# Additions in groups of eight, the first pair picked by products, and the end of a layer in another order, in a two-layer trunk with a mixture of experts

## The chip, the cores and the metric

The kernel runs on one core of a Trainium2 chip. The metric is the device time of one execution in microseconds (us), the median of several runs.

## The reference

The input x is 512 tokens of 1024 numbers. Two layers follow, each a token mixer and a channel mixer, both behind an RMS norm and added to the residual h:

```python
for i in range(2):
    xn = rms_norm(h, norm_mix[i])
    h = h + (sliding_window_attention(xn, ...) if i == 0 else gated_short_conv(xn, ...))
    h = h + hierarchical_moe(rms_norm(h, norm_ffn[i]), ...)
return rms_norm(h, final_norm)
```

Attention has 16 query and 2 key/value heads of 64 and a window of 128. The short convolution is `[B, C, u] = xn @ w_in`, `y = (B * conv3(C * u)) @ w_out`. The channel mixer picks one of 4 groups of 8 experts for each token and the two best experts in it; each of the 32 experts computes `(silu(x @ w_gate) * (x @ w_up)) @ w_down` with 512 hidden columns, and the results are weighted by the gates and summed. All numbers are float32; the weights of the 64 experts (two layers) are 6 MiB each.

## The kernel before

**Engines and order.** Each engine has its own instruction list, written by hand, and all meet on counting semaphores. Nothing reorders them: the order of the code is the order on the engine. SyncE issues the loads of weights, GpSimd the gathers of rows, TensorE (PE) the products, ScalarE (ACT) and VectorE (DVE) take the results out of the eight PSUM banks.

**Experts.** `experts(l)` exists on every engine. It runs over 16 pairs of experts (`PAIRS`); a pair has 64 slots for each of its two experts (`BLOCK`), so 128 rows. For pair i:

- `select` (L1653, VectorE) writes a 0/1 matrix token x slot from the ranks; `index` (L1121, TensorE, 68 columns) multiplies it by a table and gives the token number, the norm's root and the gate of each slot; `find_pair` takes them out.
- GpSimd's `gather` (L601) fetches the 128 rows of h from DRAM into `picked`. There is one such buffer, so the gather of the next pair waits until `turn_picked` (L1128, eight transposes) has read the last one. `take` (L1685) scales the turned rows into `xg`.
- `gate_up` (L1155) multiplies them by the gate and up weights in four groups of 16 matmul records (an fp32 matmul is two records; the two experts run at once on the two column halves of the array). `last_quarter` is the fourth group.
- `swish`, `hidden` (L1695), `turn_hidden` (L1173) and `take_hidden` (L795) make the turned hidden rows; `down` (L1180) multiplies them by the down weights in two halves, `down_first` and `down_last`, with `turn_picked` of the next pair between them.
- `take_high` (L804) and `take_low` (L1710) split the scaled result in two fp32r parts, `spread` (L1141) and `find_slots` (L1704) make the way back from slots to tokens, and `combine` (L1147, four matmuls) gives what is added to one tile of 128 tokens. VectorE adds it to h (L1747). The four tiles of pair i-1 are combined between the four `gate_up` groups of pair i, all through banks 0 and 1.

**Weights.** A pair has six pieces of 2 MiB (`PIECES`): two for k 0 to 3 of gate/up, two for k 4 to 7, two for down. They go round nine slots (`RING`). Nine are loaded before the stage begins; each later one (L467) waits until the piece nine before it has been used: `gu_done` counts the ends of a pair's first and second half of gate/up, `down_done` those of down. So the tenth piece waits for the first `gu_done` of the layer.

**Start of the experts.** `router` ends with the ranks (L1627, L1629). Then VectorE selects pair 0, TensorE multiplies (L1121), VectorE makes the row numbers (L1659), GpSimd gathers; beside it TensorE counts (L1115), turns the ranks (L1135), multiplies the table of the gates and the index of pair 1, and runs two filler matmuls (`keep_busy`, L901) before it turns the picked rows and starts `gate_up`.

**End of layer 0.** After the last pair the eight half tiles are added to h, four low halves and then four high halves (`add_last`, L1726). Each engine then reads the fullest expert's count and skips the branch for experts with over 64 tokens. TensorE turns h in 32 transposes (`turn_half`, L936), ScalarE copies them out in high parts (L674), VectorE in low parts (L1401); ScalarE (L843) and VectorE (L1839) split the weights of the convolution's column blocks in high and low parts, block 0 step by step, block 1 as a whole. `split_product` (L943) then runs over eight blocks, block j from the j-th split on. ScalarE's order is: split 0, four even copies, splits 1 to 3, four odd copies, splits 4 to 7, four roots (L659), the eight splits of block 1.

**End of layer 1.** `norm(4)` takes four tiles: ScalarE the roots (L659), VectorE the product with root and gain (L1392), SyncE stores.

## Time and profile before

| | us |
|---|---|
| median of 3 runs | 1353.9 (1350.97 to 1355.2) |
| the profiled execution | 1351.3 |
| its span, first to last instruction | 1349.4 |
| TensorE busy | 1294.5 (96%) |
| VectorE busy | 578.0 (43%) |
| ScalarE busy | 256.7 (19%) |
| GpSimd busy | 110.4 (8%) |
| granted TensorE clock, mean | 0.988 |

The span is cut by the work into the attention and first router (to about 188), the experts of layer 0 (199 to 661), the convolution and second router (667 to 865), the experts of layer 1 (875 to 1340) and the last norm. An engine that is busy 96% of the span can still wait for something at the one place that sets the end of a stage, so the table alone does not say what bounds the kernel. A matmul's busy time is partly modelled; start to start of a long group is the safer reading.

### The profile page before, as it was taken

The numbers are of one execution on the slowest core, as the hardware profiler recorded it, in microseconds if no ns is written. First come the engines' busy times: TensorE is split into PE (matmuls) and PEld (weight loads), VectorE is DVE, ScalarE is ACT, GpSimd is POOL, SyncE is SP. The second block draws the span as 40 slices with busy tenths as digits, with TensorE's granted clock in tenths as the row PEclk, the third lists the DMA queues.
The fourth block names the chain that finished last, engine by engine and source line by source line (L and its number), as shares of the span: only waits on it lengthen the run. The fifth ranks groups of instructions, "written<-read, shape, count | busy, mean of one in ns | idle before, by whom it ended". The sixth has DMA issues, their size and how long they took to land.

```text
span 1349.4 us, 14705 instructions
## 1 busy us (share of the span) xinstructions
PE 1294.5 (96%) x5986; PEld 668.7 (50%) x5986; DVE 578.0 (43%) x1232; ACT 256.7 (19%) x556; POOL 110.4 (8%) x120
## 2 busy tenths in 40 slices
PE   7999989999999999999999999899999999999996
PEld 5777653344334444333588888633443333443332
DVE  5586342343343333333566661423433433433334
ACT  3257611010100111000532221110101001101002
POOL 3850010000000000000000000100000000000000
PEclk8999989999999999999999999899999999999998
DMA  9301768999999999999723337589999999999993
GB/s 346 97 1 52 307 279 357 427 427 428 426 425 427 426 426 427 426 428 428 213 94 105 113 149 294 221 342 426 427 427 427 427 426 425 427 426 426 426 428 150
DMA packets 65306, 450.73 MB, mean 334 GB/s; under 512 B 17722, under 2 KB 33108, under 8 KB 40660
## 3 DMA queue, kind: packets, MB, share of 16 engines
q1 hardware_dynamic: 58976, 436.09, 78.0%
q0 software_dynamic: 5760, 12.59, 2.5%
q8 instruction: 50, 0.82, 0.2%
q10 hardware_dynamic: 500, 1.06, 0.2%
q14 instruction: 20, 0.16, 0.0%
HBM read 451.79 MB, written 6.32 MB: 339 GB/s over the span
## 4 chain that ended last, share of the span: by engine, by line
PE 83%; DMA 10%; DVE 4%; ACT 1%; issue 1%; DVEq 0%; SPq 0%; ACTq 0%
PE ps L1155 29%; PE ps L943 20%; PE ps L1180 15%; PE ps L1147 9%; DMA big<-in_moe_w_gate_up_dram 7%; DMA small<-in_moe_w_gate_up_dram 2%; PE ps L1128 2%; PE ps L1086 1%; PE ps L901 1%; PE ps L1121 1%; PE ps L1025 1%; PE ps L1141 1%; PE ps L992 1%; ACT arena L795 1%; DVE h L1726 1%
## 5 line engine op out<-in xcount | busy, mean ns | idle before, releaser
L1155 PE MATMUL ps<-big,arena 128*64 128x512 f32 x1200 | 464.8, 597 | 5.1 <-DMA big<-in_moe_w_gate_up_dram 1.9
L1747 DVE TENSOR_TENSOR h<-ps,h 128x512 f32<-128x512 f32 x240 | 154.7, 686 | 203.7 <-PE ps L1147 203.7
L1155 PEld LDWEIGHTS ps<-big,arena 128*64 128x64 f32 x1200 | 133.5, 136 | 144.4 <-issue 143.2
L1180 PE MATMUL ps<-small,arena 128*64 128x512 f32 x336 | 152.7, 597 | 3.3 <-ACT arena L795 3.1
L1155 PE MATMUL ps<-small,arena 128*64 128x512 f32 x336 | 152.7, 597 | 1.1 <-DMA big<-in_moe_w_gate_up_dram 1.1
L1147 PE MATMUL ps<-arena_parts 128*128 128x512 f32 x512 | 151.4, 419 | 1.7 <-DVE arena_parts L1710 1.7
L1147 PEld LDWEIGHTS ps<-arena_parts 128*128 128x128 f32 x512 | 86.6, 188 | 95.6 <-issue 83.8
L943 PE MATMUL ps<-xt_parts,small_parts 128*128 128x512 f32 x288 | 111.5, 397 | 2.9 <-DVE big_parts L1839 2.9
L790 ACT ACTIVATE gain<-ps,slot_root 128x512 f32<-128x512 f32 x32 | 22.0, 688 | 477.9 <-PE ps L1155 477.9
L943 PE MATMUL ps<-xr_parts,small_parts 128*128 128x512 f32 x272 | 106.6, 392 | 0.0
L943 PE MATMUL ps<-xt_parts,big_parts 128*128 128x512 f32 x256 | 99.7, 389 | 0.0
L601 POOL DMA_INDIRECT arena<-h_rows,arena x32 | 32.4, 1012 | 801.2 <-PE ps L1128 762.4
L1685 DVE TENSOR_TENSOR arena<-ps,gffn 128x512 f32<-128x512 f32 x64 | 41.3, 686 | 118.0 <-PE ps L1128 118.0
L804 ACT ACTIVATE arena_parts<-ps,slot_gate 128x512 fp32r<-128x512 f32 x64 | 44.0, 687 | 238.7 <-PE ps L1180 238.7
L1710 DVE SCALAR_TENSOR_TENSOR arena_parts<-ps,slot_gate,arena_parts 128x512 fp32r<-128x512 f32 x64 | 48.1, 751 | 94.1 <-ACT arena_parts L804 94.1
L1180 PE MATMUL ps<-arena 128*64 128x512 f32 x176 | 79.8, 597 | 1.7 <-ACT arena L795 1.4
L1180 PE MATMUL ps<-xr,arena 128*64 128x512 f32 x176 | 79.8, 597 | 1.7 <-ACT arena L795 1.4
L1155 PE MATMUL ps<-xr,arena 128*64 128x512 f32 x176 | 79.7, 597 | 0.5 <-DMA big<-in_moe_w_gate_up_dram 0.5
L1180 PE MATMUL ps<-xt,arena 128*64 128x512 f32 x176 | 80.0, 598 | 0.0
L1155 PE MATMUL ps<-arena 128*64 128x512 f32 x176 | 79.8, 597 | 0.0
L1695 DVE SCALAR_TENSOR_TENSOR gain<-ps,slot_root,gain 128x256 f32<-128x256 f32 x64 | 37.6, 670 | 90.4 <-PE ps L1155 71.6
L1180 PE MATMUL ps<-big,arena 128*64 128x512 f32 x160 | 72.7, 597 | 3.3 <-ACT arena L795 3.1
(208 smaller groups left out, 1646.6 us busy)
## 6 DMA issues: line engine op xcount, KB each, us to landing
big<-in_moe_w_gate_up_dram SPq DMA_DIRECT2D x75, 2048.0 KB, 22.9
small<-in_moe_w_gate_up_dram SPq DMA_DIRECT2D x21, 2048.0 KB, 21.7
small<-in_moe_w_down_dram SPq DMA_DIRECT2D x21, 2048.0 KB, 24.7
arena<-in_moe_w_gate_up_dram SPq DMA_DIRECT2D x11, 2048.0 KB, 22.0
xr<-in_moe_w_down_dram SPq DMA_DIRECT2D x11, 2048.0 KB, 23.7
xt<-in_moe_w_down_dram SPq DMA_DIRECT2D x11, 2048.0 KB, 23.3
arena<-in_moe_w_down_dram SPq DMA_DIRECT2D x11, 2048.0 KB, 24.6
xr<-in_moe_w_gate_up_dram SPq DMA_DIRECT2D x11, 2048.0 KB, 22.4
```

The lines of the kernel that those rows point to most:

```text
L601: nc.gpsimd.indirect_dma_start(out=picked, out_offset=None, in_=h_dram[l], in_offset=bass.IndirectOffsetOnAxis(ap=where[:, slot:slot + 1], ...
L790: nc.scalar.activation(silu, ps[2][:], ACT.Silu, scale=slot_root[:, slot:slot + 1]).then_inc(S.silu_ready, 1)
L804: nc.scalar.activation(parts(y_high[:, c, :]), ps[6 + c][:], ACT.Copy, scale=slot_gate[:, slot:slot + 1]).then_inc(S.high_ready, 1)
L943: mm = nc.tensor.matmul(bank, parts(a), parts(b), start=start and a is left and b is right, stop=stop and a is left_low)
L1128: mm = nc.tensor.transpose(ps[d // 4][:, (d % 4) * P:(d % 4 + 1) * P], picked.rearrange("p (q k) -> p k q", k=DT)[:, d, :], ident[:])
L1147: mm = nc.tensor.matmul(ps[bank + n][:], parts(selT[:, slot, t * P:(t + 1) * P]), parts(y[:, c, :]), start=y is y_high, stop=y is y_low)
L1155: mm = nc.tensor.matmul(ps[2 + half][j * BLOCK:(j + 1) * BLOCK, :], xg[:, k, j * BLOCK:(j + 1) * BLOCK], ws[j][:, k % FT, half * FF:(half ...
L1180: mm = nc.tensor.matmul(ps[6 + c][j * BLOCK:(j + 1) * BLOCK, :], hidT[:, k, j * BLOCK:(j + 1) * BLOCK], ws[j][:, k, c * HALF:(c + 1) * HAL ...
L1685: V.tensor_tensor(xg[:, ks, :], ps[half][:].rearrange("p (a b) -> p a b", a=4), layer_gain[0][:, ks].unsqueeze(2).to_broadcast([P, 4, P]), ...
L1695: V.scalar_tensor_tensor(out=hid.rearrange("q (k p) -> q p k", p=P)[:, :, ks], in0=ps[3][:].rearrange("q (p k) -> q p k", p=P)[:, :, ks], ...
L1710: V.scalar_tensor_tensor(out=parts(y_low[:, c, :]), in0=ps[6 + c][:], scalar=slot_gate[:, slot:slot + 1], in1=parts(y_high[:, c, :]), op0= ...
L1747: ins = V.tensor_tensor(hs, ps[c][:], hs, ALU.add)
```

## The change

1. **Pairs.** `gate_up` of k 0 to 3 is one group of 32 records, then come `spread` and the additions of tiles 0 and 1 of the pair before (eight matmuls, banks 0, 1 and 6, 7), 16 records, tiles 2 and 3 (eight), the last quarter, `turn_picked` of the next pair, `index`, `turn_hidden`, and then `down` in one piece.
2. **First pair of a layer.** A second selection, plain fp32, is written to `first_sel`. `pick_first` multiplies h by it: for each of eight k, four matmuls of 128x128. This gives the picked and turned rows with no gather. Index, ranks, counts and the index of pair 1 move behind the first 32 records of `gate_up` (`first_indexes`), the filler matmuls are gone, and the gather of pair 1 is the first of the layer. The first index and the gates' index become one.
3. **End of layer 0.** VectorE reads the count before the last additions. It then adds the low halves, splits step 0, takes the even turns, splits 1, adds the high halves, splits 2 and 3, takes the odd turns and splits 4 to 7. TensorE turns the even halves, runs the first 18 products, and then turns the odd halves.
4. **End of layer 1.** GpSimd multiplies tiles 0 and 1 of h by the gain, VectorE by the root.
5. Some semaphores are merged (`rel_in` into `attn_in`, `w_o_in` into `w_out_in`, `eps_ready` into `consts_ready`).

```diff
@@ pe: first pair
+            def pick_first(S, l):
+
+                pe.wait_ge(first_selected, l + 1)
+                for k in range(DT):
+                    for t in range(TT):
+                        mm = nc.tensor.matmul(ps[k // 4][:, k % 4 * P:(k % 4 + 1) * P],
+                                              h[:, t, :].rearrange("p (q k) -> p k q", k=DT)[:, k, :], first_sel[:, t, :],
+                                              start=(t == 0), stop=(t == TT - 1))
+                    if k % 4 == 3:
+                        mm.then_inc(S.picked_turned, 1)
+
+            def first_indexes(S, l):
+
+                o = l * PAIRS
+                pe.wait_ge(S.selected, o + 1)
+                pe.wait_ge(tab_ready, l + 1)
+                index(S)
+                turn_ranks()
+                count(l)
+                pe.wait_ge(S.selected, o + 2)
+                index(S)
+                pe.wait_ge(ranks_taken, l + 1)
...
@@ pe: experts
-                pe.wait_ge(S.selected, o + 1)
-                index(S, 0, GATE)
-                count(l)
-                turn_ranks()
-                pe.wait_ge(tab_ready, l + 1)
-                index(S, GATE, TAB)
-                pe.wait_ge(S.selected, o + 2)
-                index(S)
-                keep_busy(2, 3)
-                pe.wait_ge(S.picked_in, 16 * (o + 1))
-                turn_picked(S)
+                pick_first(S, l)
...
+                    ws = weights(i, 0)
                     pe.wait_ge(S.rows_taken, 2 * n + 1)
-                    ws = weights(i, 0)
-                    gate_up(both((0, 1)), ws)
+                    gate_up(both((0, 1, 2, 3)), ws).then_inc(S.gu_done, 1)
                     if i == 0:
-                        pe.wait_ge(ranks_taken, l + 1)
+                        first_indexes(S, l)
                     spread(S, n, i)
                     if i:
-                        add_pair(i - 1, 0)
+                        add_tiles(i - 1, (0, 1))
+                    ws = weights(i, 2)
                     pe.wait_ge(S.rows_taken, 2 * n + 2)
-                    gate_up(both((2, 3)), ws).then_inc(S.gu_done, 1)
-                    if i:
-                        add_pair(i - 1, 1)
-                    ws = weights(i, 2)
                     gate_up(both((4, 5)), ws)
                     if i:
-                        add_pair(i - 1, 2)
+                        add_tiles(i - 1, (2, 3))
                     last_quarter(S, ws)
-                    if i:
-                        add_pair(i - 1, 3)
+                    if i < LAST:
+                        if i:
+                            pe.wait_ge(S.added, l * ADDS + TT * (i - 1) + 3)
+                        pe.wait_ge(S.picked_in, 16 * (l * LAST + i + 1))
+                        turn_picked(S)
...
                     turn_hidden(S, n)
                     ws = weights(i, 4)
-                    down_first(S, n, ws)
-                    if i < LAST:
-                        if i:
-                            pe.wait_ge(S.added, l * ADDS + TT * i)
-                        pe.wait_ge(S.picked_in, 16 * (n + 2))
-                        turn_picked(S)
-                    down_last(S, n, ws)
+                    down(S, n, ws)
...
@@ pe: convolution, block 0
-            for half in range(2):
-                for t in range(TT):
-                    turn_half(t, half)
+            for t in range(TT):
+                turn_half(t, 0)
...
+                        if k == 2:
+                            for t in range(TT):
+                                turn_half(t, 1)
...
@@ dve: router
+                V.tensor_tensor(first_sel.rearrange("p t (j s) -> p t j s", j=2),
+                                iota[:].unsqueeze(1).unsqueeze(1).to_broadcast([P, TT, 2, BLOCK]),
+                                rank[:, :, 0:2].unsqueeze(3).to_broadcast([P, TT, 2, BLOCK]), ALU.is_equal)\
+                    .then_inc(first_selected, 1)
                 select(main, slice(0, 2))
...
@@ dve: end of layer 0
+                def conv_begin(between_halves):
+                    split_low_of(CONV_SPLIT, 0, [0])
+                    for t in range(TT):
+                        take_turned(2, t, [0])
+                    split_low_of(CONV_SPLIT + 1, 0, [1])
+                    between_halves()
+                    for k in (2, 3):
+                        split_low_of(CONV_SPLIT + k, 0, [k])
+                    for t in range(TT):
+                        take_turned(2, t, [1])
+                    for k in range(FT, DT):
+                        split_low_of(CONV_SPLIT + k, 0, [k])
...
@@ dve: norm_tile
+                if i == 4 and t < 2:
+                    dve.wait_ge(pool_scaled, t + 1)
+                    V.tensor_scalar(xr[:, t, :], xr[:, t, :], rstd[:, t:t + 1], None, ALU.mult).then_inc(xr_ready, 1)
+                    return
...
@@ gpsimd
-                    gather(S, l, n, i % AHEAD, 2 * n if i else None)
+                    if i:
+                        gather(S, l, n, i % AHEAD, 2 * n)
+                    else:
+                        pool.wait_ge(S.index_ready, n + 1)
...
+            for t in range(2):
+                pool.wait_ge(h_ready, 2 * (TT + t + 1))
+                nc.gpsimd.tensor_tensor(xr[:, t, :], h[:, t, :], gain[:], ALU.mult).then_inc(pool_scaled, 1)
```

TensorE, start of layer 0's experts before: the last matmuls of the router, then index, counts, ranks, filler, turned rows, and the first gate products.

```order
L1107 MATMUL ps<-arena,ones 128x32
L901 MATMUL ps<-ident 128x512
L1121 MATMUL ps<-arena_parts 128x4 x4
L1115 MATMUL ps<-arena,ones 128x32 x4
L1135 MATMUL ps<-ident,rank 32x128 x4
L1121 MATMUL ps<-arena_parts 128x64 x4
L1121 MATMUL ps<-arena_parts 128x68 x4
L901 MATMUL ps<-ident 128x512 x2
L1128 MATMUL ps<-ident,arena 128x128 x8
L1155 MATMUL ps<-big,arena 64x512
```

The same place in the change (its lines are numbered anew: L1144 is `pick_first`, L1184 `gate_up`).

```order
L1113 MATMUL ps<-arena,ones 128x32
L908 MATMUL ps<-ident 128x512
L1144 MATMUL ps<-arena,h 128x128 x32
L1184 MATMUL ps<-big,arena 64x512
...
L1127 MATMUL ps<-arena_parts 128x68 x4
L1164 MATMUL ps<-ident,rank 32x128 x4
L1121 MATMUL ps<-arena,ones 128x32 x4
L1127 MATMUL ps<-arena_parts 128x68 x4
L1170 MATMUL ps<-arena_parts 128x512
```

The index products, ranks and counts have moved behind the first sixteen gate products; 32 fp32 products stand in the place of the turned rows.

VectorE, from the last additions of layer 0 to the splits of block 1, before (the branch for full experts left out).

```order
L1726 TENSOR_TENSOR h<-ps,h 128x512 x7
...
L1401 TENSOR_TENSOR xr_parts<-ps,xt_parts 128x512 x4
L1839 SCALAR_TENSOR_TENSOR big_parts<-big,gmix,small_parts 128x3x128 x4
L1401 TENSOR_TENSOR xr_parts<-ps,xt_parts 128x512 x4
L1839 SCALAR_TENSOR_TENSOR big_parts<-big,gmix,small_parts 128x3x128 x4
...
L1839 SCALAR_TENSOR_TENSOR big_parts<-big,gmix,small_parts 128x3x128 x8
```

And in the change (L1753 additions, L1671 splits, L1422 turned parts).

```order
L1753 TENSOR_TENSOR h<-ps,h 128x512 x3
L1671 SCALAR_TENSOR_TENSOR big_parts<-big,gmix,small_parts 128x3x128
L1422 TENSOR_TENSOR xr_parts<-ps,xt_parts 128x512 x4
L1671 SCALAR_TENSOR_TENSOR big_parts<-big,gmix,small_parts 128x3x128
L1753 TENSOR_TENSOR h<-ps,h 128x512 x4
L1671 SCALAR_TENSOR_TENSOR big_parts<-big,gmix,small_parts 128x3x128 x2
L1422 TENSOR_TENSOR xr_parts<-ps,xt_parts 128x512 x4
L1671 SCALAR_TENSOR_TENSOR big_parts<-big,gmix,small_parts 128x3x128 x4
...
L1671 SCALAR_TENSOR_TENSOR big_parts<-big,gmix,small_parts 128x3x128 x8
```

The four additions of the high halves have moved behind the even turned parts, and one split ahead of them. ScalarE's list is not changed here.

## Rows read from the trace of the kernel before

**Rows 1.** Busy time (us) of each engine in long stretches, clock, DMA share, GB/s

```profile
208.50:628.50 420.00, 411.57 (x1876) 166.36 (x1872) 155.04 (x284) 42.01 (x76) 18.33 (x28) 1.00 1.01 426
884.50:1305.00 420.50, 411.73 (x1876) 166.59 (x1872) 155.08 (x284) 42.29 (x76) 18.33 (x28) 1.00 1.01 426
```

**Rows 2.** The chain that ended last: start us, us, what

```profile
224.31 3.43 PE ps L1155 x16
...
583.04 1.14 PE ps L1147 x4
584.18 3.58 PE ps L1155 x16
...
598.49 30.38 DMA small<-in_moe_w_gate_up_dram
...
629.00 3.65 PE ps L1155 x16
...
684.71 144.21 PE ps L943 x636
```

**Rows 3.** Timeline of SyncE's queue, tenth piece of each layer

```profile
206.98 0.33 SPq L467 DMA_DIRECT2D big<-in_moe_w_gate_up_dram  x1
...
883.05 0.33 SPq L467 DMA_DIRECT2D big<-in_moe_w_gate_up_dram  x1
```

**Rows 4.** Timeline, start of the experts: start us, us, engine line op

```profile
187.41 0.69 DVE L1653 TENSOR_TENSOR arena_parts<-iota,rank 128x512 fp32r<-128x512 f32 x1
188.15 0.61 PE L1121 MATMUL ps<-arena_parts 128*128 128x4 f32 x4 [0.43 <-DVE arena_parts L1653]
188.62 1.06 PE L1115 MATMUL ps<-arena,ones 128*128 128x32 f32 x8
...
189.51 0.60 PE L1135 MATMUL ps<-ident,rank 128*32 128x128 f32 x4
...
199.27 0.64 PE L1155 MATMUL ps<-big,arena 128*64 128x512 f32 x1 [0.42 <-DVE arena L1685]
...
864.59 0.69 DVE L1653 TENSOR_TENSOR arena_parts<-iota,rank 128x512 fp32r<-128x512 f32 x1
```

**Rows 5.** One us of windows; the number before the last two is the granted clock

```profile
197.00:198.00 1.00, 1.00 (x3) 0.40 (x3) 0.00 (x0) 0.00 (x0) 0.00 (x0) 0.51 0.02 8
```

**Rows 6.** Turns in the timeline, and fp32 products grouped by line

```profile
660.69 3.65 PE L936 MATMUL ps<-ident,h 128*128 128x128 f32 x32
...
L1335 PE MATMUL ps<-gain,ones 128*128 128x128 f32 x8 | 1.1, 275 | 0.0
```

**Rows 7.** Landing of the gathers started at 190.0, at 221.6, and of all 32

```profile
L601 POOL DMA_INDIRECT arena<-h_rows,arena x1: 1074/1074/1074, 190.0 to 190.0; - x1
...
DMA to landing us min/median/max: 7.6/7.6/7.6
...
DMA to landing us min/median/max: 10.2/10.2/10.2
...
DMA to landing us min/median/max: 3.4/11.1/12.3
```

**Rows 8.** Timeline, end of layer 0

```profile
664.09 2.48 DVE L1401 TENSOR_TENSOR xr_parts<-ps,xt_parts 128x512 fp32r<-128x512 f32 x4 [1.23 <-ACT xt_parts L674]
664.76 2.08 ACT L674 ACTIVATE xt_parts<-ps 128x512 fp32r<-128x512 f32 x4
...
667.24 0.47 PE L943 MATMUL ps<-xt_parts,small_parts 128*128 128x512 f32 x1 [2.90 <-DVE big_parts L1839]
...
678.41 4.33 DVE L1839 SCALAR_TENSOR_TENSOR big_parts<-big,gmix,small_parts 128x384 fp32r<-128x384 f32 x8 [2.90 <-ACT small_parts L843]
```

**Rows 9.** A product on GpSimd by line, and the load of the last gain

```profile
L582 POOL TENSOR_TENSOR h<-h,arena 128x1024 f32<-128x1024 f32 x4 | 11.5, 2896 | 0.0
...
gain<-in_final_norm_dram ACTq DMA_DIRECT2D x1, 512.0 KB, 3.8
```

**Rows 10.** Timeline of VectorE in the last norm

```profile
1340.63 0.16 DVE L1387 RECIPROCAL rstd<-rstd 128x1 f32<-128x1 f32 x1 [0.89 <-ACT rstd L666]
...
1345.01 1.29 DVE L1392 SCALAR_TENSOR_TENSOR xr<-h,rstd,gain 128x1024 f32<-128x1024 f32 x1
```

More of the change, by code:

```diff
@@ L1174, in turn_hidden, with down_steps @@
                     mm.then_inc(S.turned, 1)
-            def down(S, steps, ws):
+            def down_steps(steps, ws):
                 for k, c in steps:
@@ L1641, in router, with split_low_of @@
                     .then_inc(tab_ready, 1)
-                dve.wait_ge(rank_ps, 2 * l + 2)
-                V.tensor_reduce(most_f[:], ps[7][:, 0:E], X, ALU.max).then_inc(dve_step, 1)
-                steps[0] += 1
-                dve.wait_ge(dve_step, steps[0])
-                V.tensor_copy(fullest[:, l:l + 1], most_f[:]).then_inc(route_ready, 1)
+            def split_low_of(n, j, ks):
+                dve.wait_ge(w_high, n + 1)
+                w, high = conv_weights(j)
+                for k in ks:
+                    at = slice(3 * k, 3 * k + 3)
+                    ins = V.scalar_tensor_tensor(out=parts(w[:, at]), in0=w[:, at], scalar=gmix[:, k:k + 1],
+                                                 in1=parts(high[:, at]), op0=ALU.mult, op1=ALU.subtract)
+                ins.then_inc(w_split, 1)
             layer_gain = [None]
@@ L1760, in experts, with last_halves @@
                     if i:
[L1761 to L1762 removed]
+                        add_tile(i - 1, 2, 0)
+                        add_tile(i - 1, 3, 6)
                     hidden(S, n, i % AHEAD)
[L1764 to L1768 removed]
                     if i < LAST:
                         take(S, n + 1)
[L1771 to L1773 removed]
+                    if i + 2 < PAIRS:
+                        dve.wait_ge(S.indexed, o + i + 3)
+                        find_pair(S, i + 2)
+                def last_halves():
+                    n = o + LAST
+                    count = before + ADDS
                     take_low(S, n, 0, LAST % AHEAD)
@@ L1778, in experts, with last_other_halves, last_tiles @@
                         add_last(count + t + 1, t, 0)
+                def last_other_halves():
                     for t in range(TT):
-                        add_last(count + TT + t + 1, t, 1)
-                else:
+                        add_last(before + ADDS + TT + t + 1, t, 1)
+                def last_tiles():
+                    n = o + LAST
                     for c in range(2):
@@ L1785, in experts @@
                         for c in range(2):
-                            add_last(count + 2 * t + c + 1, t, c)
-                dve.wait_ge(h_ready, 2 * TT * (l + 1))
+                            add_last(before + ADDS + 2 * t + c + 1, t, c)
+                def conv_begin(between_halves):
[10 more added lines that the diff above has]
+                        split_low_of(CONV_SPLIT + k, 0, [k])
                 dve.wait_ge(route_ready, l + 1)
```

125 lines of the change are left out of this document (56 added, 69 removed).

## The prediction

> **What bounds the kernel now.** I read the busy shares of long windows first, then the chain of waits, then the starts and ends of the stages in the timeline. TensorE is busy 96% of the span, yet in the two expert stages it is not the bound. From 208.5 to 628.5 us, and again from 884.5 to 1305, the DMA engines are at their full share at 426 GB/s [rows 1]. TensorE leads in the middle of a stage, because nine pieces of weights were loaded ahead, and has used its lead up at the end: the chain of waits runs 30.38 us through one weight transfer and comes back to TensorE at 629.00, at the last pair [rows 2]. A piece is 2.097 MB, so 4.92 us at 426 GB/s. The tenth piece, the first that needs a slot to come free, is issued at 206.98 [rows 3]; the last pair's products start 422.0 later. In layer 1 that piece goes out at 883.05. The end of an expert stage therefore hangs on when its tenth piece is issued, and on whether the queue ever runs dry behind it. Elsewhere TensorE bounds; the stretches to look at are the start of the experts and the end of layer 0.
>
> **Groups of eight, down in one piece: 0 us.** A group of 16 product records takes 3.58 between additions and 3.43 where nothing changes before it; four additions take 1.14, of which four records of 512 columns (half of 3.43/8 each) are 0.86 [rows 2]. A change to the additions and back so costs about 0.43. The change takes out two a pair, some 0.8 us, 26 over 32 pairs. I count it as nothing: TensorE only reaches its transfers earlier. Its cover is the stream of 422 us; were that gone, all 26 would show. In the last pair, behind the last transfer, two changes less are worth 0.8, but no addition lies beside the hidden rows any more, which VectorE makes in about as long. Zero.
>
> **First pair by products.** Before, the first selection of layer 0 starts at 187.41 and the first gate product at 199.27; between them lie index products, a gather and filler products [rows 4]. After: one more selection of the same shape (0.69), then 32 fp32 products, 64 records of 128x128. No such product is in the trace of before. The nearest rows are 32 turns of 128x128 in 3.65, 0.114 each, and eight fp32 records of this very shape in 1.1, 0.1375 each with their tail [rows 6]. From below, a 512-column record holds its half of the array 0.43 (eight twos in 3.43), a quarter of it is 0.107. I take 0.114, the steady one: 7.3 us (6.8 to 8.8). Start 188.15, end 195.45. The 32 records of gate products follow in 7.05 (the second half of the picked rows is only awaited later), and piece ten is issued at 202.6 instead of 206.98: 4.4 earlier. In layer 1 the selection at 864.59 gives 872.6 and 879.75 instead of 883.05: 3.3 earlier.
>
> What was ahead of the first product is now behind it, on TensorE: index 0.6, turned ranks 0.6, counts 1.06, index 0.6, together 2.9 [rows 4], then the spread (0.4) and 7.0 of products. So the next two pieces are issued 10.35 after the tenth, where two pieces last 9.83: 0.5 us of empty queue. Then TensorE stands at the picked rows of pair 1. Their gather needs the second index, whose product ends near 205.4, and starts 1.2 behind it (before: 188.76 to 190.0 [rows 4, 7]), at 206.6. Landings of before: 3.4 on an empty queue; 7.6 for the first gather, whose stream drained at about 196.5; 10.2 where new pieces came 2.8 after its start; 11.1 as the median [rows 7]. Here the pieces ahead of it drain at 202.6 + 1.5 + 9.8 = 213.9 (full traffic comes 1.5 after the issue [rows 1, 3]) and new ones come only after. That is nearest to the 7.6 row, which landed 1.1 after the drain: 215.0, a landing of 8.4. TensorE wants the rows at 212.85: **a wait of 2.2 us** that no profile of before has. Bounds: none with 3.4, 4.8 with 11.1.
>
> Behind that wait stand the turns 1.1, index 0.4, hidden turns with their wait 1.0 and down 7.05, and the issue of the next pieces. Down is done 22.1 after the tenth piece's issue, where four pieces last 19.66. The stream starts in effect 2.45 after 202.6, at 205.05: **1.95 earlier than before in layer 0**, and at 882.2 against 883.05, **0.85 earlier in layer 1**. Later gathers are issued a pair ahead and cost nothing.
>
> The Trainium skill ("DMA: Bandwidth & Descriptors", Queues, rings and completion order) says that each DMA engine goes round between the queue rows packet by packet. By that rule the gather would hardly wait for the pieces, and the sum below would be 3.9 lower. The 10.2 and 11.1 of the rows speak against it.
>
> **Tail of layer 0.** VectorE now does its first weight split and the even turns before the second half of the additions. Before: idle 1.23 behind the additions, even turns from 664.09 in 2.48, first split, convolution from 667.24 [rows 8]. After: four additions fewer ahead of them, first split to 661.0, even turns from the first copy at 661.9 to 664.4. TensorE starts 2.75 earlier. It then has 16 of the 32 turns inside the run (1.8), so block 0 ends at 683.0 instead of 683.8. But ScalarE's order is unchanged: its odd copies stand ahead of its last four splits, its four roots and the eight splits of block 1. The odd turns now come behind 18 products, at 668.6; the odd copies start at about 669.2 instead of 664.76, so the eight splits end at 682.9 instead of 678.4, and VectorE's eight (4.33) at 687.25. Block 1 waits for all of them. It began at 684.71 [rows 2, 8]: **2.6 us later**. TensorE ran 144 us without a wait from there [rows 2], so nothing gives it back. SyncE's bias and weight loads wait for all additions and move about 4.6 too, ahead of their use by as much as they lose.
>
> **Tail of layer 1.** GpSimd multiplies two tiles by the gain; its nearest product, 128x1024, takes 2.9 us [rows 9]. The gain takes 3.8 to land [rows 9], at about 1337.0, so the second tile stands at 1342.8; then VectorE needs one short product and its two full tiles, to 1346.8. Before it ended at 1346.3, after an idle 0.89 behind the branch, which now stands earlier [rows 10]. From +0.5 at this price to -0.9 if GpSimd is never awaited; I take zero. Merged semaphores: zero, since TensorE waits for weights there.
>
> **Sum**: -1.95 + 2.6 - 0.85 = -0.2, on the profiled execution's own 1351.3: 1351.1. The median of the runs is 1353.9, 2.6 above that execution; the forecast for the median is **1353.7 us**. A measurement of this kernel can tell about 0.3% (4.1 us) from no change, so: no change.
>
> **Rivals.**
> - *Full gather wait* (slower). If the gather lands as in the loaded stage, in 11.1, the wait is 4.8 and the streams start 0.65 and 1.75 later than before, not earlier: with the 2.6, +5.0, 1358.9. For it: most gathers take this long. Against: they have a backlog of four pieces or more. It decides from a landing of 10.6 on. Chance 0.19.
> - *No gather wait*: the queue lets the gather through, as the rule above has it; streams 3.9 and 2.8 earlier, tail +2.6: -4.1, 1349.8. Without the late block 1 too (its splits ready in time), -7.5, 1346.4. For it: 3.4 on an empty queue. Against: 7.6 with one and a half pieces of backlog. Chance 0.26 for the two.
> - *The products at half clock.* The granted clock was at its half level at 197 [rows 5], after sparse small products. At that level picking takes twice 7.3: +14.6, 1368. Against: before, the clock was full until 191, and TensorE is now dense from 188. Chance 0.04.
> - *TensorE is the bound after all*: -26, 1328. Against it rows 1 and 2. Chance 0.03.
>
> **Numbers.** The forecast case has 0.48 and runs from -2.9 (gather 7.6, 0.107 a record) to +4.3 (gather 9.2, 0.1375). The range takes in most of the first two rivals: 1348.0 to 1359.5. Faster by over 0.3%: half of the no-wait rival's first part, all of its second, the TensorE case and a little of the forecast, 0.25. Slower: the full wait, the half clock and the forecast's dear end, 0.25. Within: 0.50.
>
> **What would show it.** Picking: 64 records in 7 to 9 us from 188.1. In both layers a TensorE idle time of about 2 us before the turned rows of pair 1. A pair in mid-stage about 0.8 shorter, the waits for weights some pairs earlier, and the last of them 424.5 behind the issue of piece ten. An idle time near 3 us before block 1, ended by VectorE's splits. It is wrong if the last wait for weights moves by more than the stream's start does, if pair 1's rows land with TensorE still busy, or if block 1 starts before 684.

## The result, and the profile after

| | before | after |
|---|---|---|
| median, us (4 runs each) | 1352.97 (1350.97 to 1355.2) | 1374.47 (1372.02 to 1376.83) |
| ratio, 95% interval | | 1.0158 (1.0131 to 1.0185) |
| span of the profiled execution, us | 1349.4 | 1374.0 |
| mean granted clock of TensorE | 0.988 | 0.987 |

The change made the kernel 21.5 us slower. The forecast, no change in 1348.0 to 1359.5, was wrong.

The chain of waits of the kernel after holds most of it. The columns are start and length in us, then what ran. First the start of the experts in layer 0 and the last pair there:

```profile
187.20 0.70 DVE arena L1651
187.94 15.48 PE ps L1144 x64
...
214.29 9.54 DMA arena<-h_rows,arena
...
226.56 8.06 PE ps L1209 x32
...
636.53 7.09 PE ps L1184 x32
```

Picking the first pair (L1144) takes 15.48 us for 64 records, 0.242 each; the forecast had 7.3. Then the gather of pair 1 is on the chain, and the down products behind it take 8.06 where the later pairs take 7.09. The same chain in layer 1:

```profile
877.92 15.48 PE ps L1144 x64
...
904.20 11.37 DMA arena<-h_rows,arena
...
915.61 1.97 PE ps L1134 x8
...
919.34 8.13 PE ps L1209 x32
...
1329.45 7.09 PE ps L1184 x32
```

Here the gather takes 11.37, the turns behind it 1.97 instead of 1.09, and down 8.13. TensorE's timeline has the two waits, in brackets; the forecast had 2.2 for each:

```profile
223.87 1.16 PE L1134 MATMUL ps<-ident,arena 128*128 128x128 f32 x8 [3.31 <-DMA arena<-h_rows,arena]
...
915.61 1.97 PE L1134 MATMUL ps<-ident,arena 128*128 128x128 f32 x8 [5.08 <-DMA arena<-h_rows,arena]
```

SyncE's queue, from the tenth piece on, answers to [rows 3]:

```profile
210.49 0.33 SPq L466 DMA_DIRECT2D big<-in_moe_w_gate_up_dram  x1
...
220.60 0.33 SPq L466 DMA_DIRECT2D arena<-in_moe_w_down_dram  x1
...
234.66 0.33 SPq L466 DMA_DIRECT2D xr<-in_moe_w_gate_up_dram  x1
...
900.46 0.33 SPq L466 DMA_DIRECT2D big<-in_moe_w_gate_up_dram  x1
...
910.58 0.33 SPq L466 DMA_DIRECT2D xr<-in_moe_w_down_dram  x1
...
927.50 0.33 SPq L466 DMA_DIRECT2D arena<-in_moe_w_gate_up_dram  x1
```

The tenth piece goes out 3.5 later than before in layer 0 (206.98) and 17.4 later in layer 1 (883.05); it was to go out 4.4 and 3.3 earlier. Between the second and the third of these issues lie 14.1 and 16.9 us, for two pieces that last 9.8. Between these marks the DMA engines are still at their full share, by the windows (busy us of each engine, granted clock, DMA share, GB/s), which answer to [rows 1]:

```profile
216.00:636.00 420.00, 402.31 (x1872) 178.75 (x1868) 151.86 (x284) 42.29 (x76) 18.35 (x28) 1.00 1.00 423
908.00:1329.00 421.00, 401.43 (x1862) 179.06 (x1858) 152.10 (x285) 42.29 (x76) 18.36 (x28) 0.99 1.00 421
```

The end of layer 0, from the chain again, answers to [rows 8] and to the 684.71 144.21 of [rows 2]:

```profile
672.49 4.40 PE ps L950 x18
...
677.37 2.07 ACT xt_parts L681 x4
...
686.91 4.06 ACT small_parts L850 x8
691.00 4.33 DVE big_parts L1671 x8
695.37 146.09 PE ps L950 x636
```

From the odd turns on, the chain goes through ScalarE's copies, its last four splits, its roots and its eight splits of block 1, then VectorE's eight. TensorE's timeline and the windows around the start of block 1 show what that does to it (the number before the last two is the granted clock).

```profile
695.37 0.50 PE L950 MATMUL ps<-xt_parts,small_parts 128*128 128x512 f32 x1 [3.54 <-DVE big_parts L1671]
```

```profile
690.00:695.00 5.00, 1.83 (x13) 1.47 (x11) 4.00 (x8) 4.09 (x8) 0.00 (x0) 1.00 0.13 42
695.00:700.00 5.00, 4.63 (x13) 3.71 (x14) 4.79 (x10) 1.62 (x4) 0.00 (x0) 0.66 0.00 0
```

TensorE idles 3.54 us, and then the clock is down for some 3 us. The 636 records of the convolution take 146.09 instead of 144.21.

With these marks both profiled executions split into the same intervals. "Rank known" is the start of the first selection (187.41 and 864.59 before, [rows 4]; 187.20 and 877.17 after).

| interval | before | after | difference | forecast |
|---|---|---|---|---|
| start to rank known, layer 0 | 187.41 | 187.20 | -0.2 | 0 |
| rank known to tenth piece, layer 0 | 19.57 | 23.29 | +3.7 | -4.4 |
| tenth piece to last pair's products, layer 0 | 422.02 | 426.04 | +4.0 | +2.45 |
| last pair's products to block 1 | 55.71 | 58.84 | +3.1 | +2.6 |
| block 1 to rank known, layer 1 | 179.88 | 181.80 | +1.9 | 0 |
| rank known to tenth piece, layer 1 | 18.46 | 23.29 | +4.8 | -3.3 |
| tenth piece to last pair's products, layer 1 | 422.17 | 428.99 | +6.8 | +2.45 |
| last pair's products to the end | 44.18 | 44.55 | +0.4 | 0 |

They add to the 24.6 between the spans, up to rounding. Spans of single executions scatter by some us, so the experiments are compared by the medians of their runs, and their profiles by these intervals.

### The profile page after: what moved, and what is told of

It is laid out like the page before. It is cut to its first block, busy times and chain, and to the rows that moved or that the text cites. A ratio compares the mean times of both kernels' runs of the same rounds, so it can differ in the third digit from the quotient of the medians.

```text
span 1374.0 us, 14898 instructions
## 1 busy us (share of the span) xinstructions
PE 1299.1 (95%) x6082; PEld 721.4 (53%) x6082; DVE 573.1 (42%) x1234; ACT 256.9 (19%) x556; POOL 113.1 (8%) x120
## 4 chain that ended last, share of the span: by engine, by line
PE 89%; DVE 3%; issue 3%; ACT 2%; DMA 2%; SPq 0%; POOLq 0%; DVEq 0%
PE ps L1184 32%; PE ps L950 19%; PE ps L1209 17%; PE ps L1176 9%; PE ps L1134 2%; PE ps L1144 2%; DMA arena<-h_rows,arena 2%; PE ps L1092 1%; PE ps L1031 1%; PE ps L1127 1%; PE ps L1170 1%; ACT arena L802 1%; PE ps L998 1%; PE ps L1202 1%; PE ps L1018 1%
## 5 line engine op out<-in xcount | busy, mean ns | idle before, releaser
L1184 PE MATMUL ps<-big,arena 128*64 128x512 f32 x1200 | 458.6, 595 | 16.0 <-issue 16.0
L1184 PEld LDWEIGHTS ps<-big,arena 128*64 128x64 f32 x1200 | 139.6, 137 | 151.3 <-issue 151.0
L1777 DVE TENSOR_TENSOR h<-ps,h 128x512 f32<-128x512 f32 x240 | 148.9, 683 | 95.5 <-PE ps L1176 95.5
L1209 PE MATMUL ps<-small,arena 128*64 128x512 f32 x336 | 149.4, 598 | 3.3 <-ACT arena L802 3.1
L1184 PE MATMUL ps<-small,arena 128*64 128x512 f32 x336 | 150.4, 595 | 1.3 <-issue 1.3
L1176 PE MATMUL ps<-arena_parts 128*128 128x512 f32 x512 | 134.7, 405 | 1.7 <-DVE arena_parts L1737 1.7
L1176 PEld LDWEIGHTS ps<-arena_parts 128*128 128x128 f32 x512 | 91.2, 188 | 52.4 <-issue 35.1
L1731 DVE TENSOR_SCALAR arena_parts<-ps,slot_id 128x512 fp32r<-128x512 f32 x32 | 24.0, 750 | 193.0 <-PE ps L1170 193.0
L1184 PE MATMUL ps<-xr,arena 128*64 128x512 f32 x176 | 78.7, 596 | 0.5 <-issue 0.5
L1184 PE MATMUL ps<-arena 128*64 128x512 f32 x176 | 78.7, 596 | 0.5 <-issue 0.5
L1209 PE MATMUL ps<-xt,arena 128*64 128x512 f32 x176 | 78.9, 601 | 0.0
L1184 PE MATMUL ps<-xt,arena 128*64 128x512 f32 x160 | 72.8, 598 | 2.4 <-issue 2.4
L1209 PE MATMUL ps<-big,arena 128*64 128x512 f32 x160 | 70.5, 593 | 3.3 <-ACT arena L802 3.1
```

What stands on the lines that cost most here:

```text
L1176: mm = nc.tensor.matmul(ps[bank + n][:], parts(selT[:, slot, t * P:(t + 1) * P]), parts(y[:, c, :]), start=y is y_high, stop=y is y_low)
L1184: mm = nc.tensor.matmul(ps[2 + half][j * BLOCK:(j + 1) * BLOCK, :], xg[:, k, j * BLOCK:(j + 1) * BLOCK], ws[j][:, k % FT, half * FF:(half ...
L1209: mm = nc.tensor.matmul(ps[6 + c][j * BLOCK:(j + 1) * BLOCK, :], hidT[:, k, j * BLOCK:(j + 1) * BLOCK], ws[j][:, k, c * HALF:(c + 1) * HAL ...
L1731: V.tensor_scalar(parts(selT[:, slot, :]), ps[4][:], slot_id[:, 0:1], None, ALU.is_equal)\
L1777: ins = V.tensor_tensor(hs, ps[bank + c][:], hs, ALU.add)
```

## The experiments

Twelve kernels ran, in four groups, each beside the kernel before. Its medians there were 1353.99, 1352.87, 1353.3 and 1354.09.

**1. The picking with contiguous columns.** The stationary operand of a picking product is every eighth column of h. Here it is 128 neighbouring ones. The first pair of each layer so works on permuted columns, and what lies behind it gets other numbers.

```
-     h[:, t, :].rearrange("p (q k) -> p k q", k=DT)[:, k, :], first_sel[:, t, :],
+     h[:, t, k * P:(k + 1) * P], first_sel[:, t, :],
```

> The changed kernel, with the 32 picking products reading 128 neighbouring columns of h as their stationary operand instead of every eighth one (so the first pair of each layer gets other rows of its input than it should). Theory A, the stride of the stationary operand doubles a product record: the 64 records take about 7.3 us instead of 15.5 in both layers, the tenth piece goes out about 8 earlier in each, and the median falls by some 16 us, to about 1358. Theory B, an fp32 product of this shape costs 0.24 a record however its operand lies: 15.5 us stay and so does the median, 1374. The wait for the gather of pair 1 stays in both, 3 to 5 us.

Measured: 1360.71 us (10 runs), ratio 1.0056 (1.0041 to 1.0071). That is 13.8 us under the kernel after, with the order of addresses as the only edit, and 2.7 above the 1358 expected. The chain of this kernel, in both layers:

```profile
186.72 7.41 PE ps L1144 x64
...
866.88 7.41 PE ps L1144 x64
```

The 64 records take 7.41, 0.116 each, within 0.1 of the forecast's 7.3. Rank known to tenth piece is 15.22 in both layers, as forecast (15.2). The tenth piece to the last pair's products, however, takes 424.7 and 428.7, not 422: the wait for the gather is left. Picking is then still no gain over the kernel before.

**2. The price of a stride by itself.** At the end of the kernel before, series of 16 products of 128x128 fp32 with the columns of h at a stride, each product two records. They only add work.

```
+ for n in range(16):
+     nc.tensor.matmul(ps[7][:, 0:P], flat[n % 4].rearrange("p (q k) -> p k q", k=8)[:, n // 4, :],
+                      ident[:], start=True, stop=True)
...
```

> The kernel before, with eight series of 16 products of 128x128 appended on TensorE behind its last use (they change no output): fp32 with the stationary operand at stride 1, 2, 4 and 8 elements, turns at stride 1 and 8, and fp32 with the moving operand at stride 8 and 1. Theory A (stride of the stationary operand): 0.11 us a record at stride 1, growing with the stride to 0.24 at 8, turns 0.11 to 0.14 whatever the stride. Theory B (shape): 0.24 in all the fp32 series with changing weights.

One execution, with the granted clock at 1.00 throughout the series. TensorE's timeline of this kernel:

```profile
1351.18 3.73 PE L1376 MATMUL ps<-ident,h 128*128 128x128 f32 x32
1354.75 3.93 PE L1378 MATMUL ps<-ident,h 128*128 128x128 f32 x32
1358.52 7.63 PE L1380 MATMUL ps<-ident,h 128*128 128x128 f32 x32
1365.98 7.77 PE L1382 MATMUL ps<-ident,h 128*128 128x128 f32 x32
1373.59 1.91 PE L1384 MATMUL ps<-ident,h 128*128 128x128 f32 x16
1375.34 1.95 PE L1386 MATMUL ps<-ident,h 128*128 128x128 f32 x16
1377.12 7.62 PE L1388 MATMUL ps<-h,ident 128*128 128x128 f32 x32
1384.57 3.75 PE L1390 MATMUL ps<-h,ident 128*128 128x128 f32 x32
```

L1376 to L1382 have h as the stationary operand at strides 1, 2, 4 and 8: 0.117, 0.123, 0.238 and 0.243 a record. L1388 and L1390 have it as the moving operand at strides 8 and 1: 0.238 and 0.117. L1384 and L1386 are turns at strides 1 and 8, 0.119 and 0.122. So a stride of 4 or 8 elements doubles an fp32 product for the stationary operand, a stride of 8 does so for the moving one too, and a turn at stride 8 stays as it is. Theory A of the expectation held for the turns; between the strides it had a growth, where the series show one step between 2 and 4.

**3. The start of the kernel before in the kernel after.** Gather of the first pair, filler and index products as before; groups of eight, tails and norm of the change.

```
-                 pick_first(S, l)
+                 pe.wait_ge(S.selected, o + 1)
+                 index(S, 0, GATE)
...
+                 keep_busy(2, 3)
+                 pe.wait_ge(S.picked_in, 16 * (o + 1))
+                 turn_picked(S)
```

> The changed kernel with the start of a layer's experts as before it (index products first, gather, turned rows, no picking products). If the picking products and the order around them are what costs, and the grouping of a pair costs nothing because the weight stream of some 422 us bounds the stage, the last wait for weights of each layer stands 422 us behind the tenth piece again and the whole is before plus the tail of layer 0 (3 us) plus at most 2: 1356 to 1358. Rival, the grouping itself costs: 1362 or more, with the distance from the tenth piece to the last wait clearly over 422.

Measured: 1357.05 (10 runs), ratio 1.0027 (1.0017 to 1.0036), as expected. So picking as it was made costs 17.4 against this start, and with contiguous columns 3.7. The tenth piece to the last pair's products is back at 422.1 and 422.2.

**4. The indexes ahead of the picking.** This starts the gather of pair 1 on an empty DMA queue, and so takes the gather's wait away. VectorE scales the picked rows (`take`) behind the index work here, no longer ahead of it.

```
+                 first_indexes(S, l)
                  pick_first(S, l)
...
-                    if i == 0:
-                        first_indexes(S, l)
```

> The changed kernel with the index products, ranks and counts ahead of the picking products again, so that the gather of pair 1 starts about 10 us before it is needed. The tenth piece goes out about 3.5 later than in the changed kernel, but the TensorE waits of 3.3 and 5.1 us before the turned rows of pair 1 vanish and the later pieces follow without a gap. By the theory that four slots' issues hang on that wait: effective stream start 1 us earlier in layer 0, 4 earlier in layer 1, median about 1370. Rival, the wait is hidden behind the stream and only the start counts: 7 us slower, 1381.

Measured: 1379.12 (4 runs), ratio 1.0195 (1.0169 to 1.0222), near the 1381 of the rival and not the 1370 of the theory. What failed was the price of the start, not the end of the wait: the gathers of pair 1 and pair 2 in layer 0 landed in 3.3 and 11.0 us,

```profile
L600 POOL DMA_INDIRECT arena<-h_rows,arena x2: 1029/1052/1074, 196.2 to 228.4; - x2
...
DMA to landing us min/median/max: 3.3/7.2/11.0
```

and the tenth piece to the last products is 422.18 and 422.05, so the wait's 3.9 and 6.9 are gone. But rank known to tenth piece went from 23.29 to 29.8: the indexes need selections and gates on VectorE and 4.3 us of small products on TensorE (1.04, 0.85, 1.55 and 0.86), all now ahead of the first big one. I had counted on 3.5, and on TensorE alone. So the rival's number came out, but not by its reason: the wait was not hidden before, and it did go.

**5. Groups of eight and down in one piece**, on the kernel before. The kernel has part 1 of the change, and two small things with it: the merged semaphores of part 5, and VectorE's reading of the fullest expert's count ahead of the last additions, from part 3.

```
-                    gate_up(both((0, 1)), ws)
+                    gate_up(both((0, 1, 2, 3)), ws).then_inc(S.gu_done, 1)
...
-                    down_first(S, n, ws)
+                    down(S, n, ws)
```

> The kernel before with part 1 alone (additions in two groups of eight, down in one piece); start of the experts, layer 0's tail and the last norm as before. Theory: part 1 is worth nothing, since the weights' stream sets the 422 us between a layer's tenth piece and the last pair's products. Tenth piece at 207 and 883 as before, last pair's products at 629 and 1305 (+-1), 1352 to 1356 us, ratio 1.000 +-0.002. Rival (part 1 costs something that the first pair's experiments hid): last pair's products over 2 us later than 629 at the same tenth piece. Rival (TensorE bound): 26 us less in all.

Measured: 1350.13 (12 runs), ratio 0.9977 (0.9969 to 0.9986): faster by 2.7 us, under 0.3%, but with an interval that leaves out 1. The 1352 to 1356 expected is missed by 2; the stream theory holds, to 0.3 us. SyncE's queue and the chain:

```profile
205.48 0.33 SPq L467 DMA_DIRECT2D big<-in_moe_w_gate_up_dram  x1
...
880.24 0.33 SPq L467 DMA_DIRECT2D big<-in_moe_w_gate_up_dram  x1
```

```profile
627.49 7.09 PE ps L1177 x32
...
682.38 144.21 PE ps L943 x636
...
1302.07 7.09 PE ps L1177 x32
```

Tenth piece to last products is 422.01 and 421.83. The gain lies outside: the spread no longer stands before the tenth piece's release (rank known to tenth piece 18.60 and 17.97 for 19.57 and 18.46; the first gate product to the tenth piece 7.12 in both layers for 7.71 and 7.70), and from the last pair's products to block 1 it takes 54.89 for 55.71. The latter is not the last pair's own gain: its products to the first of the last eight additions take 28.80 for 28.33. Behind the additions, VectorE stood 1.23 idle before the even turned parts [rows 8], while it read the count; that idle time is gone. So part 1 by itself is worth less than the 2.7; how much, no run separates.

**6. Layer 0's new tail added to it** (the last norm stays as before).

```
-            for half in range(2):
-                for t in range(TT):
-                    turn_half(t, half)
+            for t in range(TT):
+                turn_half(t, 0)
...
+                        if k == 2:
+                            for t in range(TT):
+                                turn_half(t, 1)
```

> The last kernel (part 1 alone) with layer 0's new tail added; the last norm stays as before. Theory: the new order on ScalarE (odd copies of the turned rows ahead of splits 4 to 7, roots ahead of block 1) makes block 1's matmuls late: they begin 3 us later than in the kernel before (687 to 688 against 684.7), and the whole is 3 to 5 us longer than the last kernel, ratio to before 1.002 to 1.004. Rival: the tail costs nothing and what after lost there came from the late start: block 1 at 685, same time as the last kernel.

Measured: 1356.93 (12 runs), ratio 1.0027 (1.0017 to 1.0036), 6.8 above the fifth kernel, where 3 to 5 were expected. The last products to block 1 take 60.43 (54.89 without), the same idle of 3.54 stands before block 1, and the convolution takes 146.07 for 144.21. Block 1 begins at 689.73, not at 687 to 688. This kernel differs from the third in the last norm alone, and the two ratios are the same.

**7. The same tail with block 1 served first.** ScalarE makes splits 4 to 7 before the odd copies, and block 1 before the roots; VectorE takes block 1's low parts ahead of the zeroing and the roots.

```
-            for k in range(1, FT):
+            for k in range(1, DT):
                 split_high_of(0, [k])
             for t in range(TT):
                 take_turned(2, t, [1])
-            for k in range(FT, DT):
-                split_high_of(0, [k])
+            split_conv(1)
             for t in range(TT):
                 root(2, t)
 
-            split_conv(1)
```

> The last kernel with three moves: on ScalarE splits 4 to 7 stand ahead of the odd copies and block 1 ahead of the roots, on VectorE block 1's low parts ahead of the zeroing and roots. Theory (ScalarE's and VectorE's order makes block 1 late): block 1's matmuls begin at 682 to 685, and 3 or more us are won against the last kernel: 1350 to 1354 us, ratio to before 0.997 to 1.001. Rival (the loads of block 1's weights or TensorE itself set it): block 1 as late as in the last kernel, same time.

Measured: 1349.76 (11 runs), ratio 0.9973 (0.9964 to 0.9982), 7.2 below the sixth. The chain has no ScalarE piece in the run of products any more, and the convolution is back at its old length:

```profile
677.03 12.30 PE ps L941 x54
...
690.22 144.21 PE ps L941 x636
```

Block 1 began later than expected on the clock (690.22 against 682 to 685), since this execution's tenth piece went out at 210.99 already; from its last products on it took 56.88. That is 2.0 more than in the fifth kernel, and the stretch from block 1 to the known rank is 1.6 shorter (178.26 for 179.89). The order on the two engines was the cause; which of the three moves counts was not separated. With it mended the new tail is level with the old one (1350.13) and no better.

**8. The last norm alone**, on the kernel before.

```
+                if i == 4 and t < 2:
+                    dve.wait_ge(pool_scaled, t + 1)
+                    V.tensor_scalar(xr[:, t, :], xr[:, t, :], rstd[:, t:t + 1], None, ALU.mult).then_inc(xr_ready, 1)
+                    return
```

> The kernel before with part 4 alone (last norm: GpSimd multiplies the gain into two of the four row tiles). My forecast's term was 0 with both bounds small: 1353.5 +-1 us, ratio 1.000 +-0.001. Rival: the end of layer 1 is 1 us or more shorter or longer.

Measured: 1353.54 (12 runs), ratio 0.9994 (0.9983 to 1.0006). Nothing, as forecast.

**9 and 10. The fifth kernel without filler products.** In layer 1 they run past the landing of the first gather. The ninth kernel drops them in both layers, the tenth in layer 1 alone.

```
-                keep_busy(2, 3)
+                if l == 0:
+                    keep_busy(2, 3)
```

> Part 1 alone (as in the groups kernel), and the two filler matmuls ahead of the wait for the first pair's gather are gone in both layers. Theory: in layer 1 the filler ran from 868.3 to 871.6 at half clock while the gathered rows had landed at about 868.9, so it holds the stream back by up to 2.6 us; in layer 0 the gather landed last (196.7) and the filler cost nothing. So rank known to tenth piece falls from 18.0 to 15.5 to 17 in layer 1 and stays at 18.6 in layer 0, and the time falls by 1 to 2.5 us against the groups kernel (1350.1): 1347.5 to 1349.5. Rival: the longer idle time lets the granted clock fall for the first pair's turns and gate/up, and 1 to 4 us are lost in each layer: 1352 to 1357.

> As the last kernel, but the filler stays in layer 0 and is gone in layer 1 alone. Theory: same as the last kernel or up to 1 us below it (in layer 0 the filler only keeps the clock up through a wait for the gather). Rival: as the groups kernel or above it, if the clock falls in layer 1 too.

Measured: ninth 1351.12 (11 runs), ratio 0.9982 (0.9969 to 0.9994); tenth 1349.16 (7 runs), ratio 0.9969 (0.9957 to 0.9982). The ninth lies above its 1347.5 to 1349.5 and below its rival's 1352 to 1357, the tenth 2.0 below the ninth, where up to 1 was expected. The intervals overlap with the fifth's (0.9977), so no gain over it is shown. The chains of layer 1, of the fifth kernel (with two filler products, L901) and of the tenth, show why:

```profile
868.33 3.23 PE ps L901 x4
871.56 0.71 PE ps L1127 x4
...
873.12 7.09 PE ps L1177 x32
```

```profile
869.97 1.97 PE ps L1127 x8
...
871.96 9.13 PE ps L1177 x32
```

Without filler the turns start 1.6 us earlier on the clock and 2.7 nearer to the known rank (6.5 behind it for 9.3), but run at half clock, and the first products take 9.13 for 7.09. Rank known to tenth piece is 17.7 for 17.97: the wait's gain went into the clock. In layer 0 of the ninth kernel it is 20.85 for 18.60, since there the gather landed last anyway and only the clock was lost. From the last products to block 1 the ninth's profile has 57.01, where the same code took 54.89 and 54.93 in the fifth and the tenth: such an interval can differ by 2 us between single executions.

**11 and 12. Filler during the wait for pair 1's gather**, on the first kernel (contiguous columns): ten filler products, then four.

```
+                        if i == 0:
+                            keep_busy(10, 0)
                         pe.wait_ge(S.picked_in, 16 * (l * LAST + i + 1))
```

> The kernel of the first experiment (after's picking with contiguous columns, so the first pair gets other rows), with ten filler matmuls ahead of the wait for pair 1's gather, so TensorE does not sit idle there. Theory of the gather wait in two parts, the wait itself and the clock that falls behind it (turns 1.97 us for 1.09, down 8.50 for 7.09 in layer 1): the clock stays at 1.00, turns take 1.09 and down 7.09, and 2 us of the 6.6 that layer 1's stream lost to the wait come back; nothing in layer 0 (its clock had not fallen): 1357 to 1360 against 1360.7, ratio to before 1.003 to 1.005. Rival: the filler outlasts the gather or delays it and the time is the same or longer.

Measured: 1364.60 (5 runs), ratio 1.0091 (1.0077 to 1.0104). Missed: ten are 8.78 us where the first kernel's waits are 3.2 and 4.4, and both layers take some 430 from tenth piece to last products. The rival of this expectation held.

> As the busy wait kernel, with four filler matmuls in place of ten. The ten took 8.78 us (0.878 each) and outlasted the gather; four take 3.5 us and end about when the gather of pair 1 lands (waits of 3.3 to 4.4 us without filler). Theory (part of the gather wait's price is the clock that falls behind it): the clock stays at 1.00, in layer 1 turns take 1.09 for 1.97 and down 7.09 for 8.50, tenth piece to last pair's products falls from 428.7 to 426 to 427.5 there and stays at 424.7 in layer 0; 1358 to 1360 against 1360.7, ratio to before 1.003 to 1.005. Rival (only the wait itself counts, the weights' queue had run dry by then anyway): 428.7 again and the same time as the first experiment, 1360 to 1361.

Measured: 1357.03 (12 runs), ratio 1.0028 (1.0014 to 1.0041), 3.7 under the first kernel (the two intervals meet at 1.0041) and 1 below the 1358 to 1360 expected. Layer 1's chain, of the first kernel and of this one:

```profile
885.10 10.68 DMA arena<-h_rows,arena
...
895.82 1.97 PE ps L1134 x8
...
899.55 8.50 PE ps L1209 x32
```

```profile
887.47 11.03 DMA arena<-h_rows,arena
...
898.55 1.16 PE ps L1134 x8
...
900.91 7.09 PE ps L1209 x32
```

The gather took no less, but what follows runs at full clock, and tenth piece to last products fell from 428.65 to 426.12. In layer 0, where the clock had not fallen, it is 425.11 for 424.68. The two intervals account for 2.1 of the 3.7. The windows say what a late issue of pieces means. In the first kernel and in this one:

```profile
905.00:910.00 5.00, 5.00 (x26) 1.74 (x24) 1.50 (x2) 1.37 (x2) 0.00 (x0) 1.00 0.25 59
```

```profile
905.00:910.00 5.00, 5.00 (x26) 1.96 (x24) 1.50 (x2) 1.37 (x2) 0.00 (x0) 1.00 0.56 174
```

The DMA share falls to 0.25 and 0.56 for five us: in part of that stretch the queue was empty. With the fillers, picking with contiguous columns is level with the start of the kernel before (the third kernel's 1.0027), not better.

By medians, as ratios to before times 1353: part 1 with the count read ahead -3.1; the rest of layer 0's tail +6.8; the norm 0; picking with its gather's wait +3.9; the stride in it +13.8. That is +21.4. These are the steps from one kernel to the next (before, fifth, sixth, third, first, after), so they add up by construction; what they show is the size of each step. The fourth kernel bears out the wait, and the seventh the tail.

## Why the prediction was wrong

- **What bounds the stages: right.** Eight kernels without a late gather gave 421.8 to 422.4 us from the tenth piece to the last pair's products, with the additions in four groups or in two. A pair in mid-stage became shorter as forecast (its down products start at 255.45 and 283.37, 27.92 apart for 28.64 before), and in the later pairs TensorE stood idle ahead of its first products instead (1.26 before the last pair's, at 635.28).
- **Groups and down in one piece, "0 us": nearly right.** The fifth kernel measured -2.7. In its profile some 0.6 a layer lie in the spread's place, which I had not counted, and 0.8 in layer 0's end, by the count read ahead of the additions. The last pair itself gained nothing, as I had it.
- **First pair by products, 7.3 us (6.8 to 8.8): this step failed.** It took 15.48 in each layer. I priced the record by its shape, from turns and from products whose stationary operand lies in neighbouring columns [rows 6], and took no account of the eighth-column view in the added line. The first experiment gave 7.41 with that view gone, the second the price of the stride. The turns were the nearest row and could not warn: those of L936 in [rows 6] read neighbouring columns, and the second experiment shows that turns do not pay for the stride of 8 either. Even the half-clock rival (twice 7.3 a layer) lay under it. The miss is 8.2 us a layer, 16.4 of the profile's 24.6.
- **Wait for pair 1's gather: mechanism right, size too small.** The streams were to lose 2.45 a layer behind the tenth piece and lost 4.0 and 6.8. The landing was 9.5 and 11.4, not 8.4: the next two pieces were issued 10.1 behind the tenth, 6.3 behind the gather's start, and before it had landed. Whether that is why it landed late was not separated, nor why layer 1 is slower: four kernels with this start have 9.4 to 9.5 in layer 0 and 10.7 to 11.4 in layer 1. And I priced the wait without the clock that falls behind it. The "full gather wait" rival, 0.19, held in layer 1 (a wait of 5.08 for its 4.8) and lies further off than the forecast's landing in layer 0. The Trainium skill ("DMA: Bandwidth & Descriptors", Queues, rings and completion order) has each DMA engine alternate between queue rows by packets. Read as "the gather hardly waits" this is not what these runs show (3.3 on an empty queue in the fourth kernel, 9.4 to 11.4 behind a busy one). The no-wait rival fell; no run here looks at the packets themselves.
- **Tail of layer 0, +2.6: mechanism right, size too small.** Block 1 was 3.1 later for the reason given, and by medians the seventh kernel takes all of it back by order alone. My sentence that TensorE runs 144 us from there missed that it starts at half clock after 3.54 us of idle: +1.9. Alone, the tail cost 6.8 by medians, and 7.4 between the profiles of the fifth and the sixth kernel (5.5 up to block 1, 1.9 from there to the known rank), of which 1.6 is the lower clock in the first 18 products.
- **Tail of layer 1 and merged semaphores, 0: right.** The tail has +0.4 in the profile and a ratio of 0.9994 alone. The semaphores never ran alone; in the fifth kernel the rank is known at 186.88, for 187.41.
- **The range** held the bounds of one form of product and none for an operand view that no row showed. That was the main fault, not the only one: with the view gone the first experiment still measured 1360.7, above the 1359.5, by the gather's wait and the tail. The forecast case's own ends come to -2.7 and +4.4 when added up again, not -2.9 and +4.3.

## What to carry to other kernels

Price an added product by its operand views as well as by its shape: look for a row with the same stride, and where there is none, let the upper bound be twice the contiguous row, the factor measured here. An idle time of TensorE can cost more than itself, since what follows may run at half clock: behind 3.3 to 5.1 us of idle that was 1.0 to 3.1 us here (down 8.06 for 7.09, the convolution 146.09 and, in the first kernel, 147.32 for 144.21), and behind 3.19 us in layer 0 of the first kernel it was nothing. A filler sized to end with the wait won 3.7 us by medians on two waits of 3.2 and 4.4; one that outlasted them lost as much. When work is moved ahead on one engine, check the order on the engines that feed it; here three moves on ScalarE and VectorE were worth 7 us.

## What the runs showed of the hardware

- An fp32 product of 128x128 takes 0.117 us a record with neighbouring columns, 0.123 at stride 2, and 0.24 at strides 4 and 8 of the stationary operand. With the moving operand it is 0.117 at stride 1 and 0.238 at stride 8. A turn takes 0.12 at stride 1 and at stride 8. All this is one execution of the second experiment; the kernels themselves bear out stride 8 (0.242) and stride 1 (0.116). I had not expected the step between 2 and 4.
- The same code behind the same idle time does not always meet the same clock. The first 18 products of layer 0's tail, behind 1.90 us of idle, took 4.38 to 4.40 in the kernel after and in the first, fourth and eleventh kernels, and 5.97 to 6.01 in the third, sixth, seventh and twelfth. The granted clock over these products was 1.00 in the kernel after and 0.71 in the sixth. That is 1.6 us from one place. Each kernel was profiled once, so whether two executions of one kernel differ in the same way is not shown.
